# Threshold search with separate rounds on ScalarE and VectorE, three masks moved ahead of the attention, and the w_out copy on ScalarE, in a hybrid decoder block

## What is computed

```python
logits = jnp.einsum("bthd,bsd->bths", qib, kif) * (IDX_DIM ** -0.5)
score = jnp.einsum("bths,bth->bts", jax.nn.relu(logits), wib * (N_IDX_HEADS ** -0.5))
score = jnp.where(causal[None], score, -jnp.inf)
_, idx = lax.top_k(score, topk)          # topk = 256
valid = idx <= q_pos[None, :, None]
s = jnp.einsum("bthd,btkd->bthk", qb, kg).astype(jnp.float32) * (Dh ** -0.5)
p = jax.nn.softmax(jnp.where(valid[:, :, None, :], s, -jnp.inf), axis=-1)
```

## Time and profile before

| | |
|---|---|
| median of 3 runs | 646.16 us (646.05 to 647.65) |
| profiled execution | 645.42 us, its span 643.6 us |
| mean granted TensorE clock | 0.918 |
| busy | PE 547.3 us (85%), DVE 441.0 (69%), ACT 371.7 (58%), POOL 238.3 (37%) |

### The profile page before, as it was taken

How to read it: one execution, slowest core, us unless ns; L and a number is a source line. 1 busy time by engine, 2 the same in 40 slices (tenths; PEclk the granted TensorE clock), 3 DMA queues, 4 the chain that set the end, 5 groups by cost and what they waited for, 6 DMA issues and landing times.

```text
span 643.6 us, 8079 instructions
## 1 busy us (share of the span) xinstructions
PE 547.3 (85%) x2704; PEld 450.4 (70%) x2704; DVE 441.0 (69%) x995; ACT 371.7 (58%) x673; POOL 238.3 (37%) x207
## 2 busy tenths in 40 slices
PE   2369999979999999999999106448999999999984
PEld 2356878768778774888888005447899989888873
DVE  5985048759977597697698989977555665655532
ACT  7423155533955948686799954135465666656621
POOL 6051645322554533566664200561042222304222
PEclk9859999989999999999999755559999999999999
DMA  8950541233611111155420600020000101011011
GB/s 348 410 159 1 146 116 42 58 98 90 237 34 47 52 33 34 33 126 140 130 66 2 261 1 0 1 98 1 1 36 31 67 1 66 1 67 66 2 65 67
DMA packets 16346, 51.98 MB, mean 81 GB/s; under 512 B 3888, under 2 KB 4912, under 8 KB 15280
## 3 DMA queue, kind: packets, MB, share of 16 engines
q1 hardware_dynamic: 16304, 51.45, 25.0%
HBM read 37.81 MB, written 4.19 MB: 65 GB/s over the span
## 4 chain that ended last, share of the span: by engine, by line
PE 59%; DVE 12%; DMA 9%; ACT 7%; POOL 6%; issue 3%; SPq 3%; DVEq 0%; POOLq 0%; ACTq 0%
PE pair L1352 22%; PE pair L1452 13%; PE pair L1474 5%; PE pair L1487 5%; DMA qs<-half_lo 5%; DMA ada<-in_ada_w 4%; ACT bias_sb L843 2%; DVE bias_sb L1073 2%; PE pair L1430 2%; PE pair L1346 2%; PE pair L1404 2%; PE pair L1431 2%; PE pair L1392 2%; PE pair L1496 2%; PE pair L1393 2%
## 5 line engine op out<-in xcount | busy, mean ns | idle before, releaser
L1352 PE MATMUL pair<-h_hi,w_hi 128*128 128x512 f32 (+1 forms) x352 | 113.1, 403 | 1.5 <-DVE h_lo L1042 1.5
L1352 PE MATMUL pair<-h_lo,w_hi 128*128 128x512 f32 (+1 forms) x352 | 109.5, 393 | 0.0
L1352 PE MATMUL pair<-h_hi,w_lo 128*128 128x512 f32 (+1 forms) x352 | 109.4, 392 | 0.0
L843 ACT ACTIVATE bias_sb<-score_sb,tinies 128x1024 bf16<-128x1024 f32 (+2 forms) x93 | 95.7, 1034 | 23.2 <-DVE tinies L1088 23.1
L1277 DVE TENSOR_TENSOR pt_lo<-pair,pt_hi 128x512 fp32r<-128x512 f32 (+3 forms) x96 | 50.4, 553 | 65.4 <-ACT pt_hi L945 65.1
L1352 PEld LDWEIGHTS pair<-h_hi,w_hi 128*128 128x128 f32 (+1 forms) x352 | 65.2, 188 | 17.2 <-issue 4.7
L1352 PEld LDWEIGHTS pair<-h_lo,w_hi 128*128 128x128 f32 (+1 forms) x352 | 66.1, 188 | 15.5 <-issue 0.9
L1352 PEld LDWEIGHTS pair<-h_hi,w_lo 128*128 128x128 f32 (+1 forms) x352 | 65.7, 187 | 15.1 <-issue 0.8
L1073 DVE TENSOR_SCALAR_CACHE_REDUCE bias_sb<-score_sb,tinies 128x640 bf16<-128x640 f32 (+2 forms) x93 | 74.1, 796 | 0.0
L672 POOL TENSOR_SCALAR w_hi<-w_raw 128x1024 fp32r<-128x1024 f32 (+1 forms) x22 | 26.2, 1190 | 120.6 <-PE pair L1352 105.2
L762 POOL TENSOR_TENSOR x_res<-q_free,x_res 128x512 f32<-128x512 f32 x14 | 18.1, 1294 | 121.1 <-DVE q_free L1248 121.1
(11 more groups left out here) (196 smaller groups left out, 1294.2 us busy)
## 6 DMA issues: line engine op xcount, KB each, us to landing
w_raw<-in_w_tiles SPq DMA_DIRECT2D x21, 512.0 KB, 3.5
ada<-in_ada_w SPq DMA_DIRECT2D x8, 1024.0 KB, 17.8
x_sb<-in_x SPq DMA_DIRECT2D x8, 512.0 KB, 6.4
qs<-half_hi SPq DMA_DIRECT2D x16, 256.0 KB, 3.6
qs<-half_lo SPq DMA_DIRECT2D x16, 256.0 KB, 4.4
ada_g<-in_ada_w SPq DMA_DIRECT2D x1, 4096.0 KB, 14.1
wo_raw<-in_w_out SPq DMA_DIRECT2D x8, 512.0 KB, 6.6
x_res<-in_x SPq DMA_DIRECT2D x8, 512.0 KB, 3.3
```

The source lines that it names most:

```text
L843: nc.scalar.activation(junk[i], score_sb[:, SCORE_OFF[i]:SCORE_OFF[i] + keys_of(i)], ACT.Sign, bias=cand[:, c:c + 1], scale=-1.0, accum_ou ...
L1352: ins = nc.tensor.matmul(psum[banks[half]][0:width, :], w[b][:, k, 0:width], hh[:, k, half * HALF:(half + 1) * HALF], start=(k == 0 and p ...
```

## The change

The coupling of the rounds is undone: `update` tests and writes one column of ScalarE in two instructions in a row as soon as its count is there, and ScalarE's next count of that column waits for that alone; VectorE counts its own three columns and updates them together (`narrow_own`) in rounds of their own. The own thresholds are written by `own_threshold`, without `settle`. The masks of tiles 4, 3, 2 (with their comparisons on ScalarE, first in the order) go into the planned part, ahead of the attention loop; those of tiles 7, 6, 5 are in steps 1, 5, 9. The order of the tiles becomes 1, 0, 4, 7, 6, 5, 3, 2. The eight copies of w_out move to ScalarE, at the end of the steps 5 to 12. The planner's costs are changed with it.

```diff
-ATT = [1, 0, 7, 6, 5, 4, 3, 2]
+ATT = [1, 0, 4, 7, 6, 5, 3, 2]
-MASK_AT = {2 * c + 1: c for c in range(len(PICK))}
-WO_START = 7
+MASK_AT = {4 * c + 1: c for c in range(ACT_COLS)}
+WO_START = 5
-COUNT_US = (1.3, 1.35, 1.6)
+COUNT_US = (1.0, 0.87, 0.74)
+OWN_US = 0.5
+UPDATE_US = 0.36
+MASK_ORDER = (3, 4, 5, 0, 1, 2)
...
-            add("ACT", ("count_a", it, c), COUNT_A_US[c], 6, ("sign",), *([("count", it - 1, min(c + 1, 2))] if it else []))
+            add("ACT", ("count_a", it, c), COUNT_A_US[c], 6, ("sign",), *([("update", it - 1, c)] if it else []))
+            add("DVE", ("update", it, c), UPDATE_US, 1, ("count_a", it, c), ("prep",))
         for c in range(3):
-            need = [("prep",), (("count_a", it, c), -COUNT_US[c] + (0.2 if c < 2 else 0.8))]
-            if c or it:
-                need.append((("count", it, c - 1) if c else ("count", it - 1, 2), 0.0))
-            add("DVE", ("count", it, c), COUNT_US[c], 6, *need)
-    add("DVE", ("post",), 5.0, 6, ("count", SEARCH_BITS - 1, 2))
+            need = (("count", it, c - 1) if c else ("own", it - 1)) if c or it else ("prep",)
+            add("DVE", ("count", it, c), COUNT_US[c], 6, (need, 0.0))
+        add("DVE", ("own", it), OWN_US, 5, (("count", it, 2), 0.1))
+    add("DVE", ("post",), 5.0, 4, *[("update", SEARCH_BITS - 1, c) for c in range(ACT_COLS)])
+    add("DVE", ("own_thr",), 0.3, 4, ("own", SEARCH_BITS - 1))
+    before = []
+    for c in MASK_ORDER:
+        n = keys_of(PICK[c])
+        add("ACT", ("cmp", c), 0.5 + n / 1200, 5, ("post",) if c < ACT_COLS else ("own_thr",), *[("cmp", b) for b in before])
+        if c >= ACT_COLS:
+            add("DVE", ("mask", c), 1.0 + n / 280, 7, ("cmp", c), *[("mask", b) for b in before])
+        before = [c]
...
+                if WO_START <= g < WO_START + KC:
+                    m = g - WO_START
+                    act.wait_ge(wo_in[m], 16)
+                    nc.scalar.activation(wo_hi[:, m, :], wo_raw[:, m, :], ACT.Copy).then_inc(wo_hi_ok, 1)
...
+            def update(it, c):
+
+                dve.wait_ge(count_a, ACT_COLS * it + c + 1)
+                nc.vector.tensor_scalar(cols(c, miss), cols(c, cnt), cols(c, lim), float(bit(it)), ALU.is_gt, ALU.mult).then_inc(miss_a, 1)
+                dve.wait_ge(miss_a, ACT_COLS * it + c + 1)
+                nc.vector.tensor_scalar(icand[:, c:c + 1], cols(c, miss), bit(it) >> 1, icand[:, c:c + 1],
+                                        ALU.bitwise_xor, ALU.bitwise_xor).then_inc(cand_a, 1)
+
+            def narrow_own(it):
+
+                dve.wait_ge(counted, 3 * it + 3)
+                nc.vector.tensor_scalar(miss[:, own], cnt[:, own], 0.0, float(bit(it)), ALU.is_lt, ALU.mult).then_inc(miss_d, 1)
+                dve.wait_ge(miss_d, it + 1)
+                nc.vector.scalar_tensor_tensor(icand[:, own], miss[:, own], bit(it) >> 1, icand[:, own],
+                                               ALU.bitwise_xor, ALU.bitwise_xor).then_inc(cand_d, 1)
...
-                dve.wait_ge(compared, c + 1)
+                dve.wait_ge(compared, MASK_ORDER.index(c) + 1)
...
+                if o[0] == "count":
+                    if o[1] and o[2] == 0:
+                        dve.wait_ge(cand_d, o[1])
+                    count(ACT_COLS + o[2])
...
-                if WO_START <= g < WO_START + KC:
-
-                    m = g - WO_START
-                    dve.wait_ge(wo_in[m], 16)
-                    nc.vector.tensor_scalar(wo_hi[:, m, :], wo_raw[:, m, :], 1.0, None, ALU.mult).then_inc(wo_hi_ok, 1)
```

More of the change, by code:

```diff
@@ L442, in layer_kernel @@
         cand = tiny(6)
+        neg_thr = tiny(6)
         sign = tiny(6)
@@ L512, in layer_kernel @@
         counted = sem("counted")
-        miss_ok = sem("miss_ok")
+        miss_a = sem("miss_a")
+        miss_d = sem("miss_d")
         cand_a = sem("cand_a")
@@ L1074, in count @@
                                         accum_out=cols(c, cnt)).then_inc(counted, 1)
-            def search(it, part):
-                bit = 1 << (SEARCH_BITS - 1 - it)
-                icand = cand[:, :].bitcast(I32)
-                own = slice(ACT_COLS, len(PICK))
-                def take(c):
-                    dve.wait_ge(count_a, ACT_COLS * it + c + 1)
-                    nc.vector.tensor_scalar(cols(c, miss), cols(c, cnt), cols(c, lim), float(bit), ALU.is_gt, ALU.mult).then_inc(miss_ok, 1)
-                def narrow(c, misses):
-                    dve.wait_ge(miss_ok, 4 * it + misses)
-                    nc.vector.tensor_scalar(icand[:, c:c + 1], cols(c, miss), bit >> 1, icand[:, c:c + 1],
-                                            ALU.bitwise_xor, ALU.bitwise_xor).then_inc(cand_a, 1)
-                if part == 0:
-                    if it:
-                        dve.wait_ge(cand_d, it)
-                    count(3)
-                    take(0)
-                if part == 1:
-                    count(4)
-                    narrow(0, 1)
-                    take(1)
-                if part == 2:
-                    count(5)
-                    narrow(1, 2)
-                    dve.wait_ge(counted, 3 * it + 3)
-                    nc.vector.tensor_scalar(miss[:, own], cnt[:, own], 0.0, float(bit), ALU.is_lt, ALU.mult).then_inc(miss_ok, 1)
-                    take(2)
-                    dve.wait_ge(miss_ok, 4 * it + 3)
-                    nc.vector.scalar_tensor_tensor(icand[:, own], miss[:, own], bit >> 1, icand[:, own],
-                                                   ALU.bitwise_xor, ALU.bitwise_xor).then_inc(cand_d, 1)
-                    narrow(2, 4)
@@ new lines, in _, with bit @@
+            own = slice(ACT_COLS, len(PICK))
+            icand = cand[:, :].bitcast(I32)
+            def bit(it):
+                return 1 << (SEARCH_BITS - 1 - it)
+            def update(it, c):
[4 more added lines that the diff above has]
+                                        ALU.bitwise_xor, ALU.bitwise_xor).then_inc(cand_a, 1)
@@ new lines, in narrow_own, with own_threshold @@
+            def narrow_own(it):
[4 more added lines that the diff above has]
+                                               ALU.bitwise_xor, ALU.bitwise_xor).then_inc(cand_d, 1)
+            def own_threshold():
+                dve.wait_ge(cand_d, SEARCH_BITS)
+                nc.vector.scalar_tensor_tensor(neg_thr[:, own], cand[:, own], -1.0, sign[:, own], ALU.mult, ALU.mult).then_inc(own_thr_ok, 1)
@@ L1131, in settle @@
                 dve.wait_ge(thr_ok, 1)
-                nc.vector.scalar_tensor_tensor(neg_thr, cand[:, :], -1.0, sign[:, :], ALU.mult, ALU.mult).then_inc(thr_ok, 1)
+                nc.vector.scalar_tensor_tensor(neg_thr[:, act_cols], cand[:, act_cols], -1.0, sign[:, act_cols], ALU.mult, ALU.mult).then_inc(thr_ok, 1)
             def mask(c):
@@ L1177, in _ @@
                     prepare()
+                if o[0] == "update":
+                    update(o[1], o[2])
                 if o[0] == "count":
-                    search(o[1], o[2])
+                    if o[1] and o[2] == 0:
+                        dve.wait_ge(cand_d, o[1])
+                    count(ACT_COLS + o[2])
+                if o[0] == "own":
+                    narrow_own(o[1])
+                if o[0] == "own_thr":
+                    own_threshold()
                 if o[0] == "post":
                     settle()
+                if o[0] == "mask":
+                    mask(o[1])
                 if o[0] == "sum":
```

10 lines of the change are left out of this document (5 added, 5 removed).

## The result

The changed kernel takes **639.15 us** (median of 4 runs, 637.53 to 641.58) against 646.16 before: a ratio of 0.989, 95% interval 0.987 to 0.992. It is faster, by 7 us (1.1%) where 19 were forecast, and 1 us above the upper end of the range. The profiled execution is the longest of the four, 641.58 us with a span of 639.5; the forecast for a profiled execution was 626.4, so 15.2 us have to be found.

The account below looks back on a forecast made before the run. The search until about 378 us, VectorE's queue until 434, then TensorE set the end. Gains of 8 (search), 3 (attention start) and 8 (steps 0 to 15), 19 us, gave 627 us; 8-in-10 range 616 to 638.

Parts of the forecast that it names:

- Part 1, the rounds: Threshold search: separate rounds remove waits between VectorE and ScalarE but expose dependence, adding 20 us of VectorE time (12 to 23).
- these 14 us: Search: stall of VectorE's two three-column operations over one-column forms in 31 rounds, kept unchanged inside its busy time.
- The sum until the attention: VectorE's work, settling and 5 us of gaps put the first attention operation at 370 us for 378.25, gaining 8.
- dependence and gaps: Before the attention: 20 us of VectorE time for exposed dependence in the rounds, and 5 us of remaining gaps.
- Part 2, masks ahead: Masks of tiles 4, 3, 2 move into or just behind the search, costing VectorE 8.4 us there.
- Part 3, start of the attention: First attention operation to first weighted-value matmul: about 7 us for 9.8, with at most three comparisons in the way; gain 2.8.
- Part 4, steps 0 to 15: First weighted-value matmul to step 16: 38 us for 46.2, with fewer masks and copies on ScalarE; gain 8 (bounds 30 to 46).
- Part 5, tile order: Tile 4 third, then 7, 6, 5: nothing gained behind step 16, 2 us either way; TensorE stays gapless.
- B: Rival: TensorE's clock returns to 2.4 GHz in attention steps 0 to 15, saving 8 us more: 619 us; chance 0.14.
- C: Rival, slower: VectorE's added 28.4 us come whole in the search while its 41.6 us of waits stay: 663 us; chance 0.06.
- A: Rival: search gains nothing, VectorE still stands at late counts; attention starts at 378: 635 us, or 640; chance 0.17.
- D: Rival: own rounds end last, masks behind everything; if comparisons delay exponentials, no gain at the attention's start: 630 us; no separate chance.

Follow-up runs that it names:

- r4: The changed kernel with VectorE's own update issued column by column, six one-column operations for two three-column ones; 631.41 us.
- r14: The changed kernel with all mask comparisons ranked behind ScalarE's last evacuation of a gate slab; 639.42 us.
- r5: The changed kernel with GpSimd's two low-part subtractions left out from weight slab 6 on, output not the reference's; 628.2 us.
- r9: The kernel before the change with GpSimd's low-part subtractions left out from weight slab 6 on, output not the reference's; 638.69 us.
- r3: The changed kernel with the masks of tiles 4, 3, 2 put back, so all six are inside attention steps 1 to 11; 640.64 us.
- r2: The kernel before the change with only the w_out copy moved from VectorE to ScalarE, in steps 5 to 12; 643.27 us.

## Why the prediction was right or wrong

**What bounds the kernel.** Right. VectorE's queue sets the end until step 16; behind it the span was 209.2 to 210.2 us in every kernel run, so what was won ahead of 434 us arrived at the end, but for 1 us.

**Part 1, the rounds: the step that failed.** Its mechanism held for VectorE. Its waits went, from 20.8 to 0.3 us for counts, and a waiting operation does start 0.23 to 0.25 us after the first of its pair (191.13 to 191.36). The sign given for ScalarE, that its waits for candidates would mostly go, failed (23.9 us for 23.1). What failed in the sum is the sentence "They stay, so I keep these 14 us inside the busy time". I had read 27.3 us for two three-column forms, taken the excess over the one-column form for a property of the instruction, and carried it over to a new order. It is a property of who runs beside it. With 0.16 us each where GpSimd idles, 62 of them cost 10 us: the excess was 17 before, not 14, and 29 after. With this term taken out (r4) the time is 631.4 us, inside the forecast's range. The mean of rows 5 hid two populations, 0.16 us and up to 2; a look at single instances beside GpSimd's timeline would have shown it.

**The sum until the attention**, 370 against 385.15, term by term: own updates +12.1; settling +3.6; masks +2.7 (11.1 for 8.4); the recurrence's L1222 and its neighbour L1219, 11.9 us for 9.8 before, +2.1; work of the preparation that still lay behind 171.4 (one 1.4 us scaling), +1.4, since in this execution the clock at 140 to 150 was 0.74 for 0.88 in that of before. That is 21.9, where 15.2 are missing. The 6.7 too many came back from what I took for dependence and gaps, 25 us together: as the rest of the sum they cost some 18. That part is luck: had they cost 25, the forecast would have been further off. r14 shows the masks' term to be due to GpSimd, and r4, r5 and r9 the own updates'; that the settling's and the recurrence's terms are too is read from the timeline and the means alone. I had put bounds of 365 to 385 on this sum, but for gaps, and let the range of the time stop at an attention start of 381. Of the 15.2 us, 2.4 are the profiled execution's own: it lies that much above its median.

**Part 2, masks ahead.** The price was right where nothing stood in the way (8.48 in r14). Not weighed was the exchange: r3 has the masks inside the attention again, and its time can't be told from that of after.

**Part 3, start of the attention.** Right: 6.5 us for 7.

**Part 4, steps 0 to 15.** Right in the sum, 38.5 for 38. In its terms, the mask of tile 5 met the stall forecast, and more of it, 8.5 us in all; its scan of 768 keys (timeline of GpSimd and VectorE, after) took 3.79 us beside GpSimd's w_out splits, where the scan of 1024 keys took 2.29 undisturbed in r4:

```profile
408.19 8.55 POOL L753 TENSOR_TENSOR wo_lo<-wo_raw,wo_hi 128x1024 fp32r<-128x1024 f32 x3 [0.47 <-ACT wo_hi L994]
...
410.81 3.79 DVE L1151 TENSOR_TENSOR_SCAN rank<-tie 128x768 f16<-128x768 bf16 x1
```

The copies on ScalarE took 1.04 us each and gave time (r2: 2.9 us), so the rule weighed there lost to the stalls as the rows had said. The row of the Trainium skill cited there, "ScalarE: Activation LUTs" (Rules for kernel authors), names relu, max, min, add and mul, not copies; it bears on this one because VectorE makes its copy by a multiplication with 1.0.

**Part 5, tile order.** Right: 209.3 us behind step 16 as before, and clock 1.00 without a gap in 442 to 572.

**The rivals.** B is refuted: the clock stood at 0.50 in 385.1 to 430.2. C did not come: the waits went. A is nearest to the time (635 to 640), and for another reason than it gave; VectorE did not stand at late counts, it stood in its own instructions. D came as described: the own rounds ended last (372.8), ScalarE idled 15.3 us until the first own comparison, and part 3 gained all the same. That the change makes the kernel faster was right.

## What to carry to other kernels

When a change makes an engine the bound of a stretch, price its small instructions by single instances, not by a group's mean: a mean far above the shortest instance (here 0.42 to 0.46 against 0.16 us) was another engine's time, and it changed with the order. On VectorE beside a busy GpSimd, several one-column operations can be cheaper than one on three columns. When a stall is removed in a kernel whose order is planned, put the measured costs into the planner again: here that gave as much again (9 us, 7 of them in the search) as the removal of the stall (8 us). And before a few us between two profiles are explained, compare them up to the place where the kernels first differ: here up to 4 us stood ahead of it, and most of them were the clock.

## What the hardware showed

- Operations on 128x3 elements took 0.16 us, or up to 3.17 us under GpSimd's instructions, and then always to the end of one; a `tensor_scalar` on 128x1 elements took 0.14 to 0.22 us throughout (r4: 186 own instances, 186 of ScalarE's updates).
- Of two dependent ones, the first is let go as a GpSimd instruction ends, and the second meets the next one from its start: 1.87 and then 2.32 us. One at 281.41 was not let go at the first end and stood through two instructions.
- The larger forms are held too: a scan of 128x768 took 3.79 us beside GpSimd's w_out subtractions, one of 128x1024 undisturbed 2.29.
- Behind the same 3.2 us wait of TensorE, the clock granted in 140 to 150 us was anything from 0.71 to 1.00 from one execution to the next, and the work behind it came up to 3 us later; behind a wait of 0.4 to 0.5 us it was 1.00 in all four profiles. Leaving out GpSimd's subtractions shortened that wait, and so moved the start of the search by 5 to 7 us in both kernels.
